# The second block's attention as one stream, with projection steps inside its iterations

## The reference

```python
    kb, vb = band(k), band(v)                       # window: own block and both neighbours
    s_loc = jnp.einsum('bnqhgd,bnkhd->bhgnqk', qb, kb).astype(F32) * scale
    s_ctx = jnp.einsum('bnqhgd,bchd->bhgnqc', qb, k_ctx).astype(F32) * scale
    p_loc, p_ctx, _ = joint_softmax(s_loc, s_ctx, s_sink)
...
    outs = [jnp.einsum('bhqk,bkhd->bqhd', (p[:, 0] - lam * p[:, 1]).astype(v.dtype), v)
            for p, (_, v) in zip(probs, kv_parts)]  # difference attention: two maps
...
    logits = [(jnp.einsum('bqhd,bkhd->bhqk', q_nope, kn)
               + jnp.einsum('bqhr,bkr->bhqk', q_rope, kr)).astype(F32) * scale
              for kn, kr, _ in kv_parts]            # latent attention, 96 wide, values 64 wide
```

## Time and profile before

| | |
|---|---|
| runs | 4688.1, 4691.3, 4698.1 us, median 4691.27 |
| profiled execution | 4698.62 us, its span 4696.8 us |
| mean granted TensorE clock | 0.899 of 2.4 GHz |
| TensorE matmuls, weight loads | 4283.5 us (91%), 3542.0 us (75%) busy |
| VectorE, ScalarE, GpSimd | 1866.7 us (40%), 1418.7 us (30%), 1420.2 us (30%) busy |
| chain that ended last | PE 81%, VectorE 11%, ScalarE 3% |

### The profile page before, as it was taken

One profiled execution on the slowest core, in us unless ns is written; L12 is line 12 of the kernel. 1 busy time (PEld: TensorE's weight loads), 2 busy tenths in 40 slices (PEclk: granted clock), 3 DMA queues, 4 the chain that ended last, 5 costly groups with the idle time before them and its releaser, 6 DMA issues.

```text
span 4696.8 us, 49017 instructions
## 1 busy us (share of the span) xinstructions
PE 4283.5 (91%) x19742; PEld 3542.0 (75%) x19742; DVE 1866.7 (40%) x3083; ACT 1418.7 (30%) x2069; POOL 1420.2 (30%) x644
## 2 busy tenths in 40 slices
PE   6899998999989999899968888889999978889998
PEld 4777767777677777677757777679999857776886
DVE  4433346554533344645443344432111354443213
ACT  3222334332322333433332222322111224443222
POOL 2213543655321354365520000012232210003442
PEclk9877999999987899999986777589999978989999
DMA  2212332444321233244410000012222110002332
GB/s 89 64 41 63 110 92 72 126 130 123 90 59 41 77 114 92 77 126 130 122 58 18 19 18 18 1 36 59 62 60 63 51 30 11 10 24 68 94 94 76
DMA packets 544830, 318.44 MB, mean 68 GB/s; under 512 B 35876, under 2 KB 517471, under 8 KB 544607
## 3 DMA queue, kind: packets, MB, share of 16 engines
q1 hardware_dynamic: 544335, 314.27, 22.8%
q10 hardware_dynamic: 272, 1.05, 0.1%
HBM read 313.18 MB, written 2.10 MB: 67 GB/s over the span
## 4 chain that ended last, share of the span: by engine, by line
PE 81%; DVE 11%; ACT 3%; issue 2%; POOL 1%; DMA 1%; SPq 0%; PEldq 0%; PEld 0%; DVEq 0%; ACTq 0%
PE acc L438 22%; PE acc L440 21%; PE acc L439 21%; PE ob L854 5%; PE pt L848 4%; PE ob L1101 1%; POOL wlo L422 1%; PE ob L714 1%; DVE t L687 1%; DVE t L1926 1%; DVE t L578 1%; PE pt L674 1%; PE pt L507 1%; DVE hl L593 1%; DVE sa L1843 1%
## 5 line engine op out<-in xcount | busy, mean ns | idle before, releaser
L422 POOL TENSOR_TENSOR wlo<-wraw,whi 128x1024 fp32r<-128x1024 f32 (+5 forms) x640 | 1420.0, 2225 | 3241.2 <-ACT whi L415 3239.9
L438 PE MATMUL acc<-hh,whi 128*128 128x512 f32 (+4 forms) x3320 | 1297.5, 391 | 86.9 <-DVE hl L593 31.6
L440 PE MATMUL acc<-hh,wlo 128*128 128x512 f32 (+4 forms) x3320 | 1252.0, 377 | 0.0
L439 PE MATMUL acc<-hl,whi 128*128 128x512 f32 (+4 forms) x3320 | 1250.5, 377 | 0.0
L415 ACT ACTIVATE whi<-wraw 128x1024 fp32r<-128x1024 f32 (+5 forms) x640 | 624.1, 979 | 1014.9 <-DMA wraw<-in_ada_w 265.6
L438 PEld LDWEIGHTS acc<-hh,whi 128*128 128x128 f32 (+1 forms) x3320 | 636.8, 192 | 241.1 <-issue 83.1
L439 PEld LDWEIGHTS acc<-hl,whi 128*128 128x128 f32 (+1 forms) x3320 | 637.3, 192 | 110.5 <-issue 19.8
L440 PEld LDWEIGHTS acc<-hh,wlo 128*128 128x128 f32 (+1 forms) x3320 | 635.3, 191 | 97.9 <-issue 0.2
L1230 DVE TENSOR_TENSOR t<-acc,sq 128x768 f32<-128x768 f32 (+1 forms) x44 | 36.3, 824 | 502.2 <-PE acc L440 502.2
L438 PE MATMUL acc<-act1h,whi 128*128 128x512 f32 x528 | 209.5, 397 | 0.0
L440 PE MATMUL acc<-act1h,wlo 128*128 128x512 f32 x528 | 208.6, 395 | 0.0
(11 more groups left out here) (330 smaller groups left out, 6247.3 us busy)
## 6 DMA issues: line engine op xcount, KB each, us to landing
wraw<-in_ffn_w SPq DMA_DIRECT2D x120, 512.0 KB, 3.9
wraw<-in_w_in SPq DMA_DIRECT2D x102, 512.0 KB, 3.8
wraw<-in_ada_w SPq DMA_DIRECT2D x96, 512.0 KB, 3.9
wraw<-in_w_up SPq DMA_DIRECT2D x88, 512.0 KB, 4.1
wraw<-in_w_down SPq DMA_DIRECT2D x32, 512.0 KB, 4.5
wraw<-in_w_out SPq DMA_DIRECT2D x16, 512.0 KB, 4.1
wraw<-in_w_mkv SPq DMA_DIRECT2D x16, 512.0 KB, 4.1
wraw<-in_ab_w_in SPq DMA_DIRECT2D x14, 512.0 KB, 3.8
```

What stands on the lines that cost most here:

```text
L422: e.tensor_tensor(wlo[0:rows, s, a:b, 0:w], wraw[0:rows, s, a:b, 0:w], whi[0:rows, s, a:b, 0:w].bitcast(F32), ALU.subtract).then_inc(lo_re ...
L438: e.matmul(o, wh, xh, start=first, stop=False)
L439: e.matmul(o, wh, xl, start=False, stop=False)
L440: return e.matmul(o, wl, xh, start=False, stop=last)
```

## The change

The two `heads_...` loops become two streams (`pe_stream`, `act_stream`, `dve_stream`). The first has 72 iterations (4 turns of 12 window and 6 difference iterations), the second 64 (16 heads of 4). The remaining projections are "jobs" whose steps are spread over the iterations by a list of ticks: 15 jobs in the first stream (steps only at the last turn's window part, none at its difference part), and 28 jobs in the second (heads 2 to 15; none in its last 8 iterations). The first query slab and the first two heads are made ahead of the streams with `pe_tiles`.

- TensorE's order in an iteration is: scores of n, the turning of a finished value tile, the projection steps, transposes of n-1, scores of the second map, products of n-1 (at once, with no other work between them and the transposes but that second map).
- Projections use `acc[1]`, so all scores go to `acc[0]`; only the last 6 iterations of the first stream and the last 7 of the second use both (`"s"`). Probabilities, their transposed copy and the combination have one buffer each where they had two.
- Window attention is cut to the keys that a mask lets through: 512, 640, 640, 512 keys for the four latent blocks instead of 768 each, and 256 as before for the two context blocks. The masks are stored for 7 blocks of 128.
- The rotation's matmul and raw copy go; VectorE takes the product with `rope_c` and a `stream_shuffle` straight out of PSUM. The sign of the rotation moves into the sine table, for the first block too.
- Negation and the sink are folded into fewer small VectorE operations (`nsink`); results of difference attention are written to their place directly.

```diff
+                    scores(n, 0)
+                if before and before[3] and jobs[before[0]]["kind"] != "rope":
+                    v = jobs[before[0]]
+                    raws += 1
+                    e.wait_ge(s_raw, c.at(s_raw, raws))
+                    if v["kind"] == "kv":
+                        e.wait_ge(s_hi, c.at(s_hi, his + 1))
...
+                tick = ticks[n] if n < N else None
+                if tick:
+                    part(tick)
+                if n:
...
+                    for j in range(len(p["v"])):
+                        tr = e.transpose(ptf[:, j * P:j * P + P], src[:, j * P:j * P + P], ident[:, :])
+                    tr.then_inc(s_tr, 1)
+                if t and len(t["maps"]) == 2:
+                    scores(n, 1)
+                if n:
+                    p, s = its[n - 1], (n - 1) % 2
+                    e.wait_ge(s_copied, c.at(s_copied, n))
...
+        def act_stream(e, c, its, jobs, ticks):
...
+                    e.activation(sq[:, 0, 0:w], ptf[:, 0:w], ACT.Copy).then_inc(s_copied, 1)
+                if t:
+                    exps(n, 0)
...
+                if tick and tick[3]:
+                    j = jobs[tick[0]]
+                    head(e, c)
+                    s, done = c.turn("acc"), c.next(slab_done)
+                    if j["kind"] != "rope":
+                        e.wait_ge(slab_done, done)
+                        e.activation(v3(sq[:, 1, 0:j["T"]], j["T"]), bank(s, j["T"], j["M"]), ACT.Copy).then_inc(s_raw, 1)
+                        if j["kind"] == "kv":
+                            e.activation(v3(j["hi"], j["T"]), bank(s, j["T"], j["R"]), ACT.Copy).then_inc(s_hi, 1)
...
+            def turned(j, s):
+                M, T, w, u = j["M"], j["T"], j["w"], j["t"]
+                A_ = bank(s, T, M)
+                half = nb(T)[1]
+                for i in range(nb(T)[0]):
+                    a, b = i * half, min(i * half + half, SEQ)
+                    e.tensor_tensor(w[0:M, a:b], A_[:, i, 0:b - a], rope_c[0:M, a:b], ALU.mult).then_inc(dve_step, 1)
+                    e.stream_shuffle(u[0:M, a:b], A_[:, i, 0:b - a], j["swap"]).then_inc(dve_step, 1)
...
+                release(e, s, T)
...
+        def ticks_ab():
+            for t in range(4):
+                for first, last, n in ((18 * t, 18 * t + 11, 3 if t == 0 else 2), (18 * t + 11, 18 * t + 17, 2 if t < 3 else 0)):
...
+            return spread(4 * C_HEADS, [(4 * h, 4 * h + 4, [(2 * h, 3), (2 * h + 1, 2)]) for h in range(C_HEADS - 2)])
...
-            def heads_ab(e, t):
-                pe_tiles(e, c, tiles_ab(), K8, hh, hl)
-                pe_attention(e, c, its_ab(t))
-                pe_diff(e, c, its_diff(t))
-            turns(pe, c, 4, heads_ab)
+            pe_stream(pe, c, its_ab(), jobs_ab(), ticks_ab(), hh, hl)
```

More of the change, by code:

```diff
@@ L92, in turn, with at @@
     def turn(self, what):
-        return self.count(what) % 4
+        n = self.count(what)
+        return 1 + n % 2 * 2 if self.narrow else n % 4
+    def at(self, sem, k, view=""):
+        return self.here.get((sem.name, view), 0) + k
     def count(self, what):
@@ L969, in act_diff @@
[L969 to L990, removed]
@@ new lines, in dve_stream @@
+            before = None
+            for n in range(N + 2):
+                t, tick = (its[n], ticks[n]) if n < N else (None, None)
+                if t:
+                    maxima(n, 0)
+                if n >= 2:
+                    result(n - 2)
+                if before and before[3]:
+                    j, s = jobs[before[0]], slots[before[0]]
+                    if j["kind"] != "v":
+                        his += 1
+                        e.wait_ge(s_hi, c.at(s_hi, his))
+                        if j["kind"] == "rope":
+                            e.tensor_tensor(j["lo"], j["w"][0:j["R"], 0:j["T"]], j["hi"].bitcast(F32), ALU.subtract)\
+                             .then_inc(s_ready, 1)
+                            e.wait_ge(s_ready, c.next(s_ready))
+                        else:
+                            e.tensor_tensor(j["lo"], sq[0:j["R"], 1, 0:j["T"]], j["hi"].bitcast(F32), ALU.subtract)\
+                             .then_inc(dve_step, 1)
+                    if j["kind"] != "rope":
+                        vts += 1
+                        e.wait_ge(s_vt, c.at(s_vt, vts))
+                        e.tensor_copy(j["v"].rearrange("p t d -> p (t d)"),
+                                      acc[1][:, :, :].rearrange("p b n -> p (b n)")[:, 0:len(j["tok"]) * j["n"]])\
+                         .then_inc(dve_step, 1)
+                        e.wait_ge(dve_step, c.next(dve_step, 1 + (j["kind"] == "kv")))
+                        release(e, s, j["T"])
+                        e.sem_inc(s_ready, 1)
+                        c.next(s_ready)
+                if t and len(t["maps"]) == 2:
+                    maxima(n, 1)
+                    combine(n)
+                if tick and tick[3]:
+                    j = jobs[tick[0]]
+                    slots[tick[0]], done = c.turn("slab"), c.next(slab_done)
+                    if j["kind"] == "rope":
+                        e.wait_ge(slab_done, done)
+                        turned(j, slots[tick[0]])
+                before = tick
@@ L1452, in its_diff @@
[L1452 to L1460 removed]
+                    dict(kind="v", M=P, T=TC, n=P, r0=0, tok=all_tok, v=vg[:, :, :]),
```

454 lines of the change are left out of this document (300 added, 154 removed).

## The result

The changed kernel takes 4717.81 us (median of 7 runs, 4707.04 to 4732.44) against 4693.92 (7 runs, 4688.10 to 4698.14): ratio 1.0056, 95% interval 1.0039 to 1.0073. It is slower by half a per cent. The forecast was 4602, faster, with a range that ended at 4690: wrong in sign and size. The profiled execution took 4715.65 us with a span of 4713.8.

The account below looks back on a forecast made before the run. TensorE was taken as the bound, at half clock in window attention. From the profiled 4698.6 us, -120 for the first stream and +31 for the second gave 4609.6, shifted to the runs' median: 4602 us, range 4548 to 4690.

Parts of the forecast that it names:

- the clock of the first stream: First layer's attention with projections woven in: TensorE taken to run at 2.4 GHz throughout.
- rival A: First stream: window attention stays at 1.2 GHz despite projection steps; +157 us, 4759 us, slower; chance 0.12.
- D: Second stream: clock falls at each value job; about 60 us more, near 4660; chance 0.20 shared with another rival.
- First stream, 585 to 465: First layer's attention stretch: falls from 585 to 465 us, -120, summed from turns at full clock.
- job ends of 9: First stream: TensorE waits for `acc[1]` at the ends of projection jobs, taken as 9 us per turn.
- Second stream, +31: Second layer's latent attention: 403 us against 372, with a head at 24.7 us where it was 23.2.
- The copy, 1.79 us from transposes to products: Every iteration: uncovered copy of the transposes makes this distance 1.79 us, where the old order needs 0.61.
- The value job, 3.4 us: Second stream: the step behind a key and value job waits for VectorE to empty `acc[1]`, 3.4 us per head.
- Shuffle 0.56 us: Rotated projection tiles: VectorE's shuffle of 384 columns out of PSUM taken as 0.56 us, like a PSUM copy.
- GpSimd 5 us: First stream: GpSimd splits holding up VectorE operations cost 5 us, up to 58 if all were exposed.
- Window cut: First stream's window iterations: scaled to fewer keys, 35.2 us per turn before projection steps, with no separate gain forecast.

Follow-up runs that it names:

- x1: The changed kernel with transposes of n-1 directly behind the first scores of n and projection steps behind those transposes, in both streams: 4579 us, ratio 0.9765.
- x7: x1 with eight useless 128x128x512 matmuls in TensorE's wait behind each value job: 4516 us, ratio 0.9619.
- x2: The changed kernel with four useless 128x128x512 matmuls per iteration between transposes and products: 4692 us, ratio 0.9996.
- x6: x1 with the former iteration's products ahead of the projection step behind each value job, in both streams: 4515 us, ratio 0.9615.
- x4: The kernel before with the window cut alone, order of work unchanged: 4648 us, ratio 0.9908.
- x11: The kernel before with four useless matmuls of 64 contraction rows per iteration of window attention: 4803 us, ratio 1.0233.

## Why the prediction was wrong

**The failing step is the clock of the first stream**: "I therefore take 2.4 GHz for the whole first stream." I took it from rows in which projections run in bulk, and gave the fall a chance only as rival A (window attention as a whole) and, for the second layer, D. The trace shows 0.80 in its place. That waits bring such falls is shown for one wait of the second stream (x1 against x7). For the first stream it is only made likely: x1 covered the waits for the copy there and the clock rose to 0.88, but x2, which filled them, gave 6 us, and x6 had a lower clock with no more idle time.

- *First stream, 585 to 465.* Forecast for the stretch between landmarks 590.4 - 120 = 470.4, measured 552.3: 82 too little. A clock of 0.80 means 2 x 0.20 x 552.3 = 221 us at 1.2 GHz; with TensorE busy for 0.79 of them (438.65 of 552.30) half of 175 us, some 87 us, is the clock's price (an estimate: it takes the stretch's mean busy share). Summed over windows of 0.5 us it is 93. That is the size of the miss; it leaves some 11 us by which the other terms together were too high. In turn two: window part 67 us against 52.5, difference part 74 against 54.4, with job ends of 9 forecast for both. x1 reached 454.1 us, the size forecast, but not the way forecast: its order waits less, and its clock was 0.88.
- *Second stream, +31.* Measured +58. The head was forecast at 24.7 us at full clock, and the one from 3930.77 to 3955.11 (high part to high part), inside a window at 0.99, took 24.34. But the mean of thirteen is 347.2 / 13 = 26.7. These 2.4 us x 14 = 33, less the 0.4 x 14 by which the forecast head was too long, cover the miss of 437.8 - 411.2 = 27 us. It is rival D's mechanism at about half its price; the clock fell behind eleven of the thirteen value jobs' waits.
- *The copy, 1.79 us from transposes to products.* Right: 1.72 in the rows above. TensorE waits for it in all 64 latent iterations, 0.90 us each (about 1.2 forecast), 57.6 us together. What I did not draw from it is that x1's order hides it behind the steps.
- *The value job, 3.4 us.* Mechanism right, size 2.3 to 2.5. Its larger price lay behind it: in x1, with most other waits gone, each head ran at 1.2 GHz for 10.3 us from this one on (x1 against x7: 58.5 us in thirteen heads).
- *Shuffle 0.56 us, GpSimd 5 us.* The shuffle was right: 384 columns took 586 ns. GpSimd's 5 us was of the right order at most. The last rotation sum has a median of 692 ns and a mean of 1285 over eleven, 6.5 us of holds; the sum ahead of it (L1200) has 3.7 us more and the addition of the sink (L1159) 6.2, some 16 us together. The low parts of `qd` and `kd` never exceeded 959:

```profile
L1195 DVE STREAM_SHUFFLE turn_t<-acc 128x384 f32<-128x384 f32 x11 | 6.4, 586 | 0.0
L1202 DVE TENSOR_TENSOR turn_w<-turn_w,turn_t 128x512 f32<-128x512 f32 x11 | 14.1, 1285 | 0.4
```

How much of these holds TensorE had to wait for is not shown.

The estimate of 0.45 us from the Trainium skill ("VectorE: DVE Perf Modes", the perf-mode tier table) is a quarter below the row.
- *Window cut.* It was inside the sum with everything else; alone it is 45 us (x4), as much as the first stream as a whole brought.
- *Rival A* came true in part. Where a window iteration carries steps it is mostly at 2.4 GHz, as I argued, but the part as a whole got 0.85, so 20 of its 67 us were at 1.2 GHz.

The Trainium skill ("TensorE: Matmul & The Clock Gate", What's actually happening) says that the gate goes by how busy TensorE has been. The waits of x1 and their filling in x7 agree with that; x11 does not, since TensorE is busy for 50.00 of 50.00 us there and the granted clock is 0.50. The measurement decides.

What stays open: what about a matmul, beside its rows of contraction, counts for the clock; why the same wait is followed by 1.2 GHz in every head of x1 and not in every head of the changed kernel; and why the clock of x6's first stretch is lower than x1's.

## What to carry to other kernels

When independent work is woven into a chain of small steps, put it where it covers a wait: the same steps behind the transposes instead of ahead of them were worth 139 us here. Price TensorE's clock for the order that will run, not from stretches that hold the same instructions in bulk: in x1 a wait of 1.9 us cost 4.5 us more than itself, once per head. And before weaving at all, test each part of a change alone: the window cut by itself gave as much as the whole change to the first layer.

## What the runs showed of the hardware

- In x1 a single 1.93 us wait of TensorE, behind twelve transposes, was followed by 10.3 us at 1.2 GHz all thirteen times. Eight useless 128x128x512 matmuls in it kept the clock at 0.99. In the changed kernel two of thirteen longer waits (2.53 and 2.54 us) were not followed by a fall.
- Window attention, with 64 rows of contraction in its scores, ran at 1.2 GHz with TensorE busy for 57.98 of 60 us. Four matmuls of 128 rows per iteration brought it to 2.4 GHz; the same four with 64 rows left it at 1.2, busy for 50.00 of 50 us, and the kernels lie 149 us apart.
- A VectorE shuffle of 128x384 out of PSUM takes 586 ns, one of 96x512 takes 719.
- A VectorE sum of 128x512 with both inputs in SBUF takes 0.69 us, and took 2.88 us (from 2667.39) beside a GpSimd split of 2.39 us (from 2667.34).
